# Recurrence turns, two half projections and three scalings moved into the last attention steps

## The reference

```python
h = rms_norm(x, gain) * (1.0 + scale_m) + shift_m
hq, hf, hi, hg, fq, fk, fv, ff = split(h @ w_in)
hg_out, hg_state = hgrn_mixer(...)           # recurrence, 4 heads x 128
fox_out = rms_norm(fox_attention(...), fox_out_gain)   # 8 heads x 64, blocks of 128 queries
mixed = concatenate([hg_out, fox_out]) @ w_out
x = x + gate_m * mixed
h = rms_norm(x, norm_ffn_gain) * (1.0 + scale_f) + shift_f
x = x + gate_f * moe(h, w_router, ...)       # 16 experts, 2 of one group of 4 per token
```

## Time and profile before

| | us |
|---|---|
| median of three runs | 774.0 |
| lowest and highest of them | 773.26, 776.86 |
| the profiled execution, its own time | 773.54 |
| its span, first to last instruction | 771.8 |

### The profile page before, as it was taken

The page is one execution under the profiler, slowest core; times in us unless marked ns, Lnnn a source line. Parts: engine busy times, 40 slices in busy tenths (PEclk is TensorE's granted clock), DMA queues, the critical chain, the costliest instruction groups (busy, mean ns, idle before and its releaser), DMA issues. The chain is left out here.

```text
span 771.8 us, 19078 instructions
## 1 busy us (share of the span) xinstructions
PE 672.2 (87%) x7455; PEld 442.2 (57%) x7455; DVE 381.8 (49%) x1053; ACT 210.1 (27%) x425; POOL 216.3 (28%) x336
## 2 busy tenths in 40 slices
PE   2999999999987969998899992699999999999920
PEld 1686476444443858665764552566666666676710
DVE  3300024200189788666645438455555555555556
ACT  4310137000161132266401110123232222232203
POOL 1212100100397620120100000234444444444440
PEclk9999999999998879999899996699999999999975
DMA  8973082536303110490095129699999999999624
GB/s 334 400 270 109 1 327 89 240 113 256 128 2 113 71 32 2 147 380 21 8 408 230 54 82 368 266 417 414 414 416 416 414 411 411 406 410 410 238 69 183
DMA packets 38417, 182.95 MB, mean 237 GB/s; under 512 B 5912, under 2 KB 6312, under 8 KB 22672
## 3 DMA queue, kind: packets, MB, share of 16 engines
q1 hardware_dynamic: 29968, 158.88, 52.0%
q0 software_dynamic: 8384, 23.12, 8.4%
HBM read 169.57 MB, written 15.28 MB: 240 GB/s over the span
## 5 line engine op out<-in xcount | busy, mean ns | idle before, releaser
L1757 PE MATMUL bank<-weights,x_hT 128*128 128x512 f32 x256 | 113.3, 601 | 0.0
L1741 PE MATMUL bank<-x_hT,weights 128*128 128x272 f32 x384 | 92.5, 403 | 0.0
L2046 PE MATMUL bank<-weights,R 128*32 128x256 f32 x1408 | 80.6, 379 | 5.1 <-issue 4.0
L1741 PEld LDWEIGHTS bank<-x_hT,weights 128*128 128x128 f32 x384 | 74.2, 195 | 16.9 <-issue 0.8
L1757 PEld LDWEIGHTS bank<-weights,x_hT 128*128 128x128 f32 x256 | 48.7, 192 | 60.4 <-issue 60.2
L845 POOL DMA_INDIRECT y_d<-R,x_hT x44 | 50.9, 1156 | 98.0 <-DVE R L1609 46.6
L2046 PEld LDWEIGHTS bank<-weights,R 128*32 128x32 f32 x1408 | 54.2, 110 | 28.5 <-issue 7.3
L1087 ACT ACT_TABLE_LOAD x44 | 56.5, 1283 | 21.0 <-DVEq L1190 20.3
L839 POOL DMA_INDIRECT R<-h_d,x_hT x46 | 48.0, 1044 | 45.8 <-POOL x_hT L858 25.4
L1087 ACT ACTIVATE R<-bank 128x128 f32<-128x128 f32 x44 | 12.2, 278 | 175.9 <-PE bank L2046 175.9
L1975 PE MATMUL bank<-weights,x_hT 128*128 128x512 f32 x128 | 58.3, 608 | 0.0
(11 more groups left out here) (346 smaller groups left out, 994.5 us busy)
## 6 DMA issues: line engine op xcount, KB each, us to landing
weights<-in_w_ada SPq DMA_DIRECT2D x24, 1024.0 KB, 11.1
weights<-in_w_exp_gate SPq DMA_DIRECT2D x16, 1024.0 KB, 10.6
weights<-in_w_exp_down SPq DMA_DIRECT2D x16, 1024.0 KB, 11.3
weights<-in_w_exp_up SPq DMA_DIRECT2D x16, 1024.0 KB, 11.3
R<-in_w_exp_down SPq DMA_DIRECT2D x16, 1024.0 KB, 11.1
weights<-in_w_in SPq DMA_DIRECT2D x7, 2048.0 KB, 8.6
R<-in_w_exp_up SPq DMA_DIRECT2D x8, 1024.0 KB, 10.9
R<-in_w_exp_gate SPq DMA_DIRECT2D x8, 1024.0 KB, 10.9
```

The source lines that it names most:

```text
L1741: ins = T.matmul(bank[b][:, 0:HALF], w[:, k, h * P:(h + 1) * P], hT[:, k, c * HALF:(c + 1) * HALF], start=(n == 0), stop=(n == KT - 1))
L1757: ins = T.matmul(bank[b][:, :], hT[:, k, i * P:(i + 1) * P], w[:, k, :], start=(k == 0), stop=(k == KT - 1))
L2046: ins = T.matmul(bank[2][32 * j:32 * j + 32, 0:2 * P].rearrange("p (w f) -> p w f", w=2), XT[:, k, :], W2[:, :, k, j * P:(j + 1) * P], sta ...
```

## The change

- The value cache and turned keys are laid further back in `hT`, so that `hT[:, 0:4]` is free during the attention's last steps.
- The list `fox` gets new entries: `m00` after the second to last value step, `m10` and `m20` after the last, then (behind `ob4`) `m30`, `m40`, `mfT`, and the first halves (contraction tiles 0 to 3) of `y40` and of `y00`. `keep_busy` is left out there.
- DVE makes root and scaling in two portions: `fox_scale(0, 3)`, blocks 3, 2 and 1, right behind the copy of block 0's `fo`, in the sample block's second step; `fox_scale(3, 5)` behind the attention, where all five stood.
- The attention's rows are turned in the order 3, 2, 1, 0, 4, through banks 0 and 2 instead of 1 and 3; `y40` goes to bank 1 and `y00` to bank 3.
- `y40`'s second half stands where the whole stood; `y00`'s first half is gone from the loop.

The diff, with the moved definition of `project` left out:

```diff
--- before.py
+++ after.py
@@ -140,8 +140,8 @@
         ckS = view(W, 4 * SLOT, FH, PAST + NDEC)
         fgain = view(W, 4 * SLOT + 2304, HW)
         kc = view(hflat, 0, 2, HW)
-        vc = view(hflat, D, 2, HW)
-        kcT = view(hflat, 2 * D, 4, PAST)
+        vc = view(hflat, 4 * TOK, 2, HW)
+        kcT = view(hflat, 4 * TOK + D, 4, PAST)
         lf = view(W, 6656, 800)
         pp = [view(W, 512 * n, 512) for n in range(4)]
         pT = [view(W, 2048 + 512 * n, 4, P) for n in range(4)]
@@ -233,6 +233,8 @@
                     grp(f"ho{i}", 4, "dve")
                     grp(f"S{i}", 5, "dve")
         QT = [3, 2, 1, 0, 4]
+        TURN = [3, 2, 1, 0, 4]
+        YB = {(i, c): 4 + (2 * i + c + 1) % 4 for i in range(4) for c in range(2)} | {(0, 0): 3}
         steps_of = [(n_q, q, c) for n_q, q in enumerate(QT) for c in range(4)]
         fox = []
         for s in range(len(steps_of) + 3):
@@ -242,8 +244,13 @@
                 fox.append(("t", *steps_of[s - 1]))
             if 1 < s <= len(steps_of) + 1:
                 fox.append(("v", *steps_of[s - 2]))
+            if s == len(steps_of):
+                fox.append(("m", 0, 0, 0))
+            if s == len(steps_of) + 1:
+                fox += [("m", 0, 1, 0), ("m", 0, 2, 0)]
             if s > 2 and s % 4 == 2:
                 fox.append(("o", *steps_of[s - 3]))
+        fox += [("m", 0, 3, 0), ("m", 0, 4, 0), ("mf", 0, 0, 0), ("y", 0, 4, 0), ("y", 0, 0, 0)]
         for kind, n_q, q, c in fox:
             if kind == "s":
                 if n_q == 3 and c == 0:
@@ -258,12 +265,13 @@
                 grp(f"fo{q}", 6, "dve")
             if kind == "o":
                 grp(f"ob{q}", 7, "dve")
-        for i in range(NTILE):
-            grp(f"m{i}0", (0, 2)[i % 2], "act")
-        grp("mfT", 4, "act")
-        for i in range(NTILE):
-            grp(f"m{i}1", (1, 3)[i % 2], "dve")
-        grp("y40", 4, "dve")
+            if kind == "m":
+                grp(f"m{q}0", (0, 2)[q % 2], "act")
+            if kind == "mf":
+                grp("mfT", 4, "act")
+        for i in TURN:
+            grp(f"m{i}1", (0, 2)[i % 2], "dve")
+        grp("y40", 1, "dve")
         grp("shift_lg", 2, "dve")
         for i in range(4):
             for c in range(2):
@@ -274,7 +282,7 @@
                     grp(f"lg{FFN[i]}", 3 - i % 2, "dve")
                     if i == 3:
                         grp("r30", 0, "act")
-                grp(f"y{i}{c}", 4 + (2 * i + c + 1) % 4, "dve")
+                grp(f"y{i}{c}", YB[i, c], "dve")
         grp("r31", 1, "act")
         grp("lg3", 3, "dve")
         grp("pos", 6, "dve")
@@ -1020,6 +1028,15 @@
                 nb = q + 1 if q < 4 else 3
                 L = (q + 1) * P if q < 4 else PAST + NDEC
                 buf = 2 * (c % 2)
+                if kind == "m":
+                    filled(act, f"m{q}0")
+                    read("act", f"m{q}0", A.copy(hT[:, 0:4, q * P:q * P + n],
+                                                 bank[(0, 2)[q % 2]][:, :].rearrange("p (k t) -> p k t", k=4)[:, :, 0:n]))
+                if kind == "mf":
+                    filled(act, "mfT")
+                    read("act", "mfT", A.copy(mfT, bank[4][:, 0:5 * KT].rearrange("p (r k) -> p r k", k=KT)))
+                if kind == "o" and q == 4:
+                    fox_squares(4)
                 if kind == "s":
                     if n_q == 3 and c == 0:
                         for j in range(2):
@@ -1041,17 +1058,6 @@
                     read("act", f"t{q}{2 * c}", ins)
                     if n_q and c == 2:
                         fox_squares(n_q - 1)
-            fox_squares(4)
-            for i in range(NTILE):
-                n = ROWS[i]
-                filled(act, f"m{i}0")
-                if i == 0:
-                    filled(act, "ob4")
-                read("act", f"m{i}0", A.copy(hT[:, 0:4, i * P:i * P + n],
-                                             bank[(0, 2)[i % 2]][:, :].rearrange("p (k t) -> p k t", k=4)[:, :, 0:n]))
-            filled(act, "mfT")
-            read("act", "mfT", A.copy(mfT, bank[4][:, 0:5 * KT].rearrange("p (r k) -> p r k", k=KT)))
-
             def square_x2(m):
                 i = FFN[m]
                 n = ROWS[i]
@@ -1424,6 +1430,15 @@
 
             dve.wait_ge(s_ckr, 48)
 
+            def fox_scale(first, stop):
+
+                dve.wait_ge(s_fq, stop)
+                rstd(st[:, 85 + first:85 + stop], st[:, 80 + first:80 + stop], HW)
+                for n_q in range(first, stop):
+                    i = QT[n_q]
+                    n, c = ROWS[i], 85 + n_q
+                    V.scalar_tensor_tensor(foxo[0:n, i, :], foxo[0:n, i, :], st[0:n, c:c + 1], fgain[0:n, :], ALU.mult, ALU.mult).then_inc(s_fo, 1)
+
             def fox_normalise(n_q):
 
                 q = QT[n_q]
@@ -1465,18 +1480,16 @@
                 if kind == "v" and c == 3:
                     filled(dve, f"fo{q}")
                     read("dve", f"fo{q}", V.tensor_copy(oT[:, :, 0:n], bank[6][:, :].rearrange("p (a b) -> p a b", a=4)[:, :, 0:n]))
+                if kind == "v" and n_q == 3 and c == 3:
+                    fox_scale(0, 3)
                 if kind == "o":
                     fox_normalise(n_q)
-            dve.wait_ge(s_fq, NTILE)
-            rstd(st[:, 85:90], st[:, 80:85], HW)
-            for i in range(NTILE):
-                n, c = ROWS[i], 85 + QT.index(i)
-                V.scalar_tensor_tensor(foxo[0:n, i, :], foxo[0:n, i, :], st[0:n, c:c + 1], fgain[0:n, :], ALU.mult, ALU.mult).then_inc(s_fo, 1)
-            for i in range(NTILE):
+            fox_scale(3, NTILE)
+            for i in TURN:
                 n = ROWS[i]
                 filled(dve, f"m{i}1")
                 read("dve", f"m{i}1", V.tensor_copy(hT[:, 4:8, i * P:i * P + n],
-                                                    bank[(1, 3)[i % 2]][:, :].rearrange("p (k t) -> p k t", k=4)[:, :, 0:n]))
+                                                    bank[(0, 2)[i % 2]][:, :].rearrange("p (k t) -> p k t", k=4)[:, :, 0:n]))
 
             dve.wait_ge(s_mod1, 80)
 
@@ -1499,7 +1512,7 @@
                 i = FFN[m]
                 filled(dve, f"y{i}{c}")
                 dve.wait_ge(s_x2, 2 * m + c)
-                read("dve", f"y{i}{c}", V.tensor_tensor(gt, bank[4 + (2 * i + c + 1) % 4][:, :],
+                read("dve", f"y{i}{c}", V.tensor_tensor(gt, bank[YB[i, c]][:, :],
                                                         mod1[:, 0, c * 512:(c + 1) * 512], ALU.mult))
                 taken(dve, f"y{i}{c}")
                 xs = x[:, i, c * 512:(c + 1) * 512]
@@ -1534,7 +1547,7 @@
                 if c:
                     dve.wait_ge(s_x2, 1)
                 for j in (2 * c, 2 * c + 1):
-                    ins = V.tensor_tensor(gt[0:32, (j % 2) * 256:(j % 2) * 256 + 256], bank[4][32 * j:32 * j + 32, 0:256],
+                    ins = V.tensor_tensor(gt[0:32, (j % 2) * 256:(j % 2) * 256 + 256], bank[1][32 * j:32 * j + 32, 0:256],
                                           mod1[0:32, 1, j * 256:(j + 1) * 256], ALU.mult)
                 if c == 0:
                     vlink(dve, ins)
@@ -1883,6 +1896,26 @@
                         output_and_state(i)
 
 
+            def project(i, c, ks):
+                if ks[0] == 0:
+                    begin(f"y{i}{c}")
+                b = bank[YB[i, c]]
+                for k in ks:
+                    ins = T.matmul(b[:, :], hT[:, k, i * P:(i + 1) * P], wslot(f"wo{k // 2}", D)[:, k % 2, c * 512:(c + 1) * 512],
+                                   start=(k == 0), stop=(k == KT - 1))
+                if ks[-1] == KT - 1:
+                    end(f"y{i}{c}", ins)
+
+            def project_sample(ks):
+                if ks[0] == 0:
+                    begin("y40")
+                for k in ks:
+                    for j in range(4):
+                        ins = T.matmul(bank[1][32 * j:32 * j + 32, 0:256], hT[:, k, SEQ:], wslot(f"wo{k // 2}", D)[:, k % 2, j * 256:(j + 1) * 256],
+                                       start=(k == 0), stop=(k == KT - 1))
+                if ks[-1] == KT - 1:
+                    end("y40", ins)
+
             for kind, n_q, q, c in fox:
                 n = ROWS[q]
                 qc = slice(q * P, q * P + n)
@@ -1923,6 +1956,20 @@
                     ins = fox_values(pe, T, n_q, q, c)
                     if c == 3:
                         end(f"fo{q}", ins)
+                if kind == "m":
+                    turned(f"m{q}0", (0, 2)[q % 2], G[:, q, :], n, 4)
+                if kind == "mf":
+                    begin("mfT")
+                    pe.wait_ge(s_mrow, 48)
+                    end("mfT", T.transpose(bank[4][:, 0:5 * KT], mrow[0:40, :], ident[0:40, 0:40]))
+                if kind == "y":
+                    taken(pe, "m40")
+                    for k in range(2):
+                        loaded(pe, f"wo{k}")
+                    if q == 4:
+                        project_sample(range(0, 4))
+                    else:
```

(48 more changed lines are left out.)

## The result

The changed kernel took 780.16 us (median of seven runs, 776.04 to 782.62), the kernel before 774.0: the ratio is 1.0071, 95% interval 1.0044 to 1.0098. A second set of runs of the same pair gave 1.0056 (1.0034 to 1.0078). By these ratios the change costs 0.6 to 0.7 per cent, 4.3 to 5.5 us; the medians lie 6.2 and 5.6 us apart. The forecast was 775.8 (772.4 to 779.2): right in sign, 4.4 us short as a time, and the range did not hold it.

What follows compares the result with a forecast made beforehand. A DVE, ScalarE and PE chain bounds the edited stretch; everything behind 401 us is rigid, so r40's start counts. +5.9 (T) - 5.05 (back) + 1.45 (half clock) = +2.3 on 773.54: 775.8 us, range 772.4 to 779.2.

Steps and rivals of the forecast that it cites:

- the insertion: On DVE right behind fo0's copy: fox_scale(0, 3) finds no gap and delays the chain by 4.4 to 4.8 us, taken as 4.6.
- T: End of ob4, the attention's last transposes, 376.92 us in before; forecast 5.9 us later at half clock, 4.7 at full clock.
- from T: DVE done, PE done with the halves: Behind the attention: DVE finishes root and two scalings at T + 5.9, PE the halves of y40 and y00 at T + 7.85.
- from T: first, last eviction: Behind m31 and m21: first eviction at T + 8.55, the five end at T + 12.1.
- from T: shift_lg starts: Behind y40's second half: shift_lg waits about 1 us for DVE's modulated router weights and starts at T + 15.15.
- from T: r40 starts: First x2 transposes, behind shift_lg: at T + 19.05 against T + 24.1 in before, so 5.05 us come back.
- r40 to the router, over before's 7.67: From r40 on: the half-clock spell of before falls on r40 and y00's second half, costing 1.45 us.
- rival (c): Ahead of ob4: the inserted scaling is hidden, T moves only some 1 us; 771.1 us, at full clock 769.7; chance 0.10.
- the gap that I blamed: PE standing still about 4 us between the last pair's scores and the third pair's transposes, expected to bring half clock.
- keep_busy at nothing: Between the attention's turns: removing its idle matmuls was priced at nothing, since the evictions set the pace there.
- rival (a): From PE's idle gap to the end of y00's half: clock stays low; 777.5 us and more, 779.5 with a long spell; chance 0.22.
- Half clock in the tail: End of the attention up to T: 1.2 GHz expected, so T moves +5.9 us instead of +4.7 at full clock.

Runs made afterwards that it cites:

- e2: Kernel before with only root and scaling split in two (blocks 3, 2, 1 behind fo0's copy, two behind the attention): 776.07 us, ratio 1.0025.
- e11: Kernel before with shift_lg's small records spread between the matmuls of y00's two halves: 772.54 us, ratio 0.9967.
- e1: Changed kernel with root and scaling of all five blocks in one portion behind the attention: 776.11 us, ratio 1.003.
- e12: e8 with the change's split scaling put back: 97.81 us from fo0's copy to the last router matmuls, 3.68 more than e8.
- e8: e7 with two idle matmuls ahead of each attention turn and shift_lg spread between y00's second and y01's first half: 772.38 us, ratio 0.9958.
- e5: Changed kernel with m00, m10, m20 moved behind ob4: 101.76 us from fo0's copy to the last router matmuls (changed 102.03).
- e10: Kernel before without the idle keep_busy matmuls between the ten turns: 98.78 us from fo0's copy to the last router matmuls (before 97.48).
- e7: Changed kernel with one scaling behind the attention, m00 and m40 among the value steps, m10 to m30 behind the halves, long modulations late: 776.5 us, ratio 1.0025.
- e9: Changed kernel with shift_lg's records spread between y00's second and y01's first half: 98.75 us from fo0's copy to the last router matmuls (changed 102.03).
- e3: Changed kernel with idle matmuls on PE ahead of the third sample pair's transposes, the projection halves and shift_lg: 776.07 us, ratio 1.0014.
- e6: Changed kernel with DVE's two long modulations behind the sample rows' update: 100.98 us from fo0's copy to the last router matmuls (changed 102.03).

## Why the prediction was wrong, step by step

The mechanism was right (the insertion is paid on DVE's chain, and less comes back behind T), and it is the sum that was 2.25 us short, nearly all of it in what the half clock takes. With a right sum the forecast would have been 778.1, inside its range; the rest of the 4.4 us is 0.46 from starting at the profiled execution instead of the median, and 1.6 that no profile locates.

| step, as the prediction put it | forecast | measured |
|---|---|---|
| insertion on DVE | 4.4 to 4.8 | 4.37 |
| T later by | 5.9 (at most 6.5) | 6.60 |
| from T: DVE done, PE done with the halves | 5.9, 7.85 | 5.90, 7.78 |
| from T: first, last eviction | 8.55, 12.1 | 8.42, 12.08 |
| from T: shift_lg starts | 15.15 | 15.16 |
| from T: r40 starts (before 24.04) | 19.05 | 20.10 |
| r40 to the router, over before's 7.67 | 1.45 | 1.89 |
| sum | +2.3 | +4.55 |

**Right.** The insertion delays T by 3 to 4 us where two profiles have the clock's fall at the same place (2.93 by e2 against e11, 3.22 by e1, 3.92 by e12 against e8), so nothing hides it; rival (c), that it is hidden, is wrong. What is behind 405 us shifts as a block. Everything from T to shift_lg's start came within 0.13 us. GpSimd, SP and the bank changes cost nothing that shows.

**Wrong: the terms at half clock, three times on the low side.** Ahead of T (+0.70): of the insertion I let 0.65 come back and held the rest of the chain unchanged at half clock, 3.95 together; against the profile of before e2 shows 4.32; the third and fourth pairs' turns at half clock (0.74 against 0.49) fit that, as they take back what the wait gives. The turns I put at 1.95, taking m20 to overlap with the copies; they took 2.29 (T at 15.26 against 12.97 in e5). And the clock had fallen at 368.2, before the gap that I blamed for it. shift_lg (+1.05): I took it at 3.9 from its start to r40, with the fall behind it; the clock fell 2.2 us into it, and it took 4.94. Behind r40 (+0.44): I took over the spell of before, 3.4 us long; this one lasted 6.8. The remaining 0.06 is T to r40 in before, 24.04 and not 24.1.

By e5, turns that stand behind T cost the halves nearly as much as they save ahead of it, so what the sum missed and an order could have spared is the second place: the spell around shift_lg.

**Without a price: keep_busy at nothing.** I said that the evictions set the pace there and that the clock was the only risk, and gave it no price. In the changed kernel none shows: the clock is up from 15.5 to 32.6 us behind fo0, through all of the attention's turns. In other orders it has one: 2.31 us up to shift_lg in e10, and in e7 y40's second half at 3.53 us where e8, with idle matmuls ahead of it, has 1.93.

**Wrong: rival (a)'s place.** I looked for the low clock in the early halves. They ran at full clock; it stood ahead of them, in the tail, and behind them, from shift_lg on. e9 puts 3.3 us on the second place.

**Wrong: the range.** Of its two ends only the terms were priced, not the kernel's own scatter: fo0 alone moves by 4.65 us between profiles of the same code, and the time before ranged from 769.26 to 779.14 us in one set of runs. A forecast of the median has to leave room for that too. 4.55 us is 0.59%: at the bound of half a per cent I should have been at even chances, not at 0.21.

Half clock in the tail was the right choice, but it did not hang on the gap: the clock fell ahead of the gap, fell without it (e1), and fell with it filled (e3), where T stayed. The costlier spell, around shift_lg, came without any wait ahead of it too (e6). So the rule of the Trainium skill that spoke against the change (TensorE: Matmul & The Clock Gate, Why this matters for your kernels: no idle gaps between bursts of matmuls) pointed the right way, though no run here ties these falls to such a gap.

What stays open: why the tail's clock falls earlier in some profiles than in others with the same code (T at 8.66, 9.34 and 10.05 in before, e10 and e11), and how often each comes, was not tried; with one profile of most kernels, differences of a microsecond between their stretches can be this alone. Nor is it shown why no half clock followed shift_lg's stretch in e2 and e10.

## What to carry to other kernels

Work that is put into a chain of waits between engines is paid for if the engine it is put on has no gap at that very place, however idle that engine is on the whole; look for the gap in its order of time, not in its busy share. When matmuls are moved together to fill a wait, price the pieces that are left behind as well: a short stretch of small matmuls may, with no wait ahead of it, bring the clock down for some microseconds (3.4 to 6.8 here). Compare profiles from a common mark just ahead of the edit, look first where the clock fell in each, and keep the scatter ahead of that mark for the range.

## What the runs showed of the hardware

- During shift_lg's 32 records (128x16) in one stretch, or up to 1.6 us behind them, the clock fell in seven of nine orders (all but e2 and e10); spread between matmuls of 512 columns it did not (e8, e9, e11, e12), although the spread order takes more PE time in itself (0.52 us for each four records, 4.2 us in all, against 3.7).
- The same 32 records took 3.71 us at 2.4 GHz and 5.01 with the last 2.8 us at 1.2; half of y40 1.93 and 3.42; eight f32 records of 512 columns 3.70 and, in before, 5.07 with the clock up for its last part.
- With the same work on PE up to 2.9 us behind fo0, the clock fell 1.7 to 2.1 us behind fo0 in eight profiles and 5.0 to 6.6 us in five. With the code of before, T came at 10.05, 9.34 and 8.66 us for falls at 1.7, 5.0 and 6.6.
- Twenty idle records of 96 columns in PE's gap (e3) did not prevent the fall: it came 8.4 us behind fo0.
